# Gate phase G0 of a hybrid decoder layer: head outputs in pairs, merges and low weight halves on VectorE, projection passes ordered by token half

## The reference, cut to what matters

```python
h = rmsnorm(x, norm1_g)
proj = h @ w_in
...
y_a = silu(layernorm(ca, conf_ln_g, conf_ln_b)) @ conf_w_out
...
# ssd(), 16 heads, chunks of 128 tokens
decay = exp(where(causal, a_t[..., :, None] - a_t[..., None, :], -inf))
mix = cb[:, :, :, None] * decay
y_diag = einsum('bcgrij,bcjgrp->bcigrp', mix, xdt)
y_off = einsum('bclgn,bcgrpn,bclgr->bclgrp', cr, h_in, exp(a_cs))
...
gates = sigmoid(h @ w_gate + b_gate).reshape(n, t, 3, D_MODEL)
mixed = gates[:, :, 0] * y_a + gates[:, :, 1] * y_b + gates[:, :, 2] * y_c
x = x + mixed @ w_o
```

## Time and profile before

| | |
|---|---|
| median of 3 runs | 1107.23 us (1105.44 to 1108.96) |
| profiled execution | 1112.5 us, span 1110.6 us, mean clock of TensorE 0.961 |
| chain that ended last | TensorE 84% of the span, VectorE 12% |
| idle time of TensorE in stage G0, 314.2 to 435.46 us | 1.5 us |

### The profile page before, as it was taken

How to read it: one execution, slowest core, us unless ns; L and a number is a source line. 1 busy time by engine, 2 the same in 40 slices (tenths; PEclk the granted TensorE clock), 3 DMA queues, 4 the chain that set the end, 5 groups by cost and what they waited for, 6 DMA issues and landing times.

```text
span 1110.6 us, 19697 instructions
## 1 busy us (share of the span) xinstructions
PE 1060.9 (96%) x8110; PEld 1036.2 (93%) x8110; DVE 598.6 (54%) x834; ACT 374.0 (34%) x585; POOL 378.8 (34%) x255
## 2 busy tenths in 40 slices
PE   5999999899999999998999898999999999999996
PEld 5999989799998989988899898999999999999996
DVE  4799879966545676766301456543442003444454
ACT  4322256443524554311423212433332123333210
POOL 3200000000135444343466643544442445444340
PEclk9999899899999999886999999999999999999997
DMA  7322216212212314233224332133222233222122
GB/s 241 115 92 81 76 58 69 60 58 76 76 56 81 119 49 132 77 126 125 72 76 156 96 95 76 39 96 94 76 71 71 86 114 104 85 76 69 62 67 81
DMA packets 42461, 97.95 MB, mean 88 GB/s; under 512 B 14496, under 2 KB 15392, under 8 KB 42400
## 3 DMA queue, kind: packets, MB, share of 16 engines
q1 hardware_dynamic: 42400, 97.08, 28.9%
HBM read 89.13 MB, written 7.93 MB: 87 GB/s over the span
## 4 chain that ended last, share of the span: by engine, by line
PE 84%; DVE 12%; ACT 1%; POOL 1%; issue 1%; DMA 0%; SPq 0%; DVEq 0%; POOLq 0%
PE accs L379 75%; DVE ca L1324 2%; DVE temps L1387 2%; PE misc L1055 1%; DVE w_split L318 1%; PE misc L899 1%; PE misc L1058 1%; PE misc L893 1%; DVE temps L1696 1%; DVE branch L1801 1%; PE misc L906 1%; PE misc L1022 1%; PE misc L1068 1%; POOL w_split L318 0%; PE misc L1041 0%
## 5 line engine op out<-in xcount | busy, mean ns | idle before, releaser
L379 PE MATMUL accs<-h_split,w_split 128*128 128x272 f32 x4992 | 652.4, 293 | 7.1 <-POOL h_split L568 4.3
L379 PEld LDWEIGHTS accs<-h_split,w_split 128*128 128x128 f32 x4992 | 644.4, 192 | 12.5 <-POOL h_split L568 5.4
L318 POOL TENSOR_TENSOR w_split<-w_raw,w_split 128x1024 fp32r<-128x1024 f32 (+3 forms) x128 | 290.5, 2280 | 422.8 <-ACT w_split L313 422.8
L379 PE MATMUL accs<-branch,w_split 128*128 128x272 f32 x2208 | 290.4, 292 | 5.7 <-DVE branch L1801 3.6
L379 PEld LDWEIGHTS accs<-branch,w_split 128*128 128x128 f32 x2208 | 284.5, 191 | 9.7 <-DVE branch L1801 4.6
L313 ACT ACTIVATE w_split<-w_raw 128x1024 fp32r<-128x1024 f32 (+3 forms) x168 | 160.3, 963 | 201.2 <-PE accs L379 201.2
L1324 DVE SCALAR_TENSOR_TENSOR ca<-part,params,ca 128x512 f32<-128x512 f32 x120 | 83.5, 746 | 0.4
L1854 DVE TENSOR_TENSOR xbc<-accs,xbc 128x544 f32<-128x544 f32 x16 | 11.6, 725 | 94.7 <-PE accs L379 94.7
L1801 DVE TENSOR_TENSOR branch<-mixed,branch 128x544 fp32r<-128x544 f32 x8 | 16.3, 2100 | 80.9 <-ACT branch L834 80.9
L318 DVE TENSOR_TENSOR w_split<-w_raw,w_split 128x1024 fp32r<-128x1024 f32 (+1 forms) x40 | 44.9, 1126 | 27.2 <-ACT w_split L313 27.1
L682 ACT ACTIVATE temps<-accs 128x272 f32<-128x272 f32 (+2 forms) x102 | 25.5, 325 | 95.2 <-PE accs L379 95.2
(11 more groups left out here) (225 smaller groups left out, 777.0 us busy)
## 6 DMA issues: line engine op xcount, KB each, us to landing
w_raw<-in_ffn_w_up SPq DMA_DIRECT2D x44, 512.0 KB, 3.6
w_raw<-in_w_in_main SPq DMA_DIRECT2D x28, 512.0 KB, 3.5
w_raw<-in_w_gate SPq DMA_DIRECT2D x24, 512.0 KB, 3.6
w_raw<-in_ffn_w_down SPq DMA_DIRECT2D x16, 384.0 KB, 3.0
w_raw<-in_ffn_w_down SPq DMA_DIRECT2D x16, 320.0 KB, 2.9
xbc<-in_x SPq DMA_DIRECT2D x16, 272.0 KB, 5.3
w_raw<-in_w_in_z SPq DMA_DIRECT2D x8, 512.0 KB, 3.6
w_raw<-in_ssm_w_out SPq DMA_DIRECT2D x8, 512.0 KB, 3.7
```

Of the source, the lines that this page charges most:

```text
L318: e.tensor_tensor(w_split[:, s, 1, 0:n], w_raw[:, s, 0:n], w_split[:, s, 0, 0:n].bitcast(F32), ALU.subtract).then_inc(w_lo[s], 1)
L379: mm = pe.matmul(accs[:, a, half, 0:HALF], w_split[:, s, wp, k * P:(k + 1) * P], rhs(s, k, xp, half), start=(first and k == 0 and n == 0), ...
```

## The change

- `pe_quad` issues the three products of an input block for the first token half, then for the second.
- `y_pair` takes the place of `y_head`: per chunk the matmuls of the even and the odd head alternate. The table has heads in twos only, and the output comes two slots after the spread. Decays and decayed C have four buffers (`head_decay`, `c_dec`); the two new ones of `c_dec` lie in `u_sb`, where the second sample state goes, so its load moves behind the last head.
- VectorE reads G0's second accumulator itself and adds the product to `mixed` (`merge_second`), and makes the low weights of G0's quads 1 to 3 and of Z's quad 0 (`g0_slot`). GpSimd's merge of G0 and ScalarE's copy go.
- ScalarE takes the exponentials of the spreads of a slot first, then those of the differences.

```diff
-HEADS_AFTER = (0, 0, 0, 0, 0, 1, 1, 2, 1, 2, 1, 2, 2, 1, 2, 1)
+HEADS_AFTER = (0, 0, 0, 0, 0, 2, 2, 0, 2, 2, 2, 0, 2, 2, 2, 0, 0)
...
-        (c_dec,) = carve(ca_flat, (P, 2, SEQ))
+        c_dec = [half[:, r] for half in (carve(ca_flat, (P, 2, SEQ))[0], carve(u_flat[:, D:2 * D], (P, 2, SEQ))[0])
+                 for r in range(2)]
...
+        def head_decay(h):
+            return T(2 + h % 4, SEQ)
...
-                    for n, (wp, xp) in enumerate(((0, 0), (0, 1), (1, 0))):
-                        for half in range(2):
+                    for half in range(2):
+                        for n, (wp, xp) in enumerate(((0, 0), (0, 1), (1, 0))):
...
             load_h0(0)
-            load_h0(1)
             load_phase(sp, "Z")
             sp.wait_ge(sem("y_head"), HEADS)
+            load_h0(1)
...
             for s in range(SLOTS):
                 split_lo(pool, ph["G0"], 0, s)
-            merge("G0", 0)
...
-                    elif g != 2:
+                    elif g == 1:
                         wait(act, sem("merged"), j + n0)
...
                 for h in groups[4 * i + s]:
                     act.wait_ge(sem("diff"), h + 1)
-                    act.activation(T(4 + h % 2, SEQ), T(4 + h % 2, SEQ), ACT.Exp).then_inc(sem("pair_decay"), 1)
-                    if h >= 2:
-                        act.wait_ge(sem("y_head"), h - 1)
-                    act.activation(c_dec[:, h % 2], misc[:, h % 2], ACT.Exp).then_inc(sem("a_exp"), 1)
+                    if h >= 4:
+                        act.wait_ge(sem("y_head"), h - 3)
+                    act.activation(c_dec[h % 4], misc[:, h % 2], ACT.Exp).then_inc(sem("a_exp"), 1)
+                for h in groups[4 * i + s]:
+                    act.activation(head_decay(h), head_decay(h), ACT.Exp).then_inc(sem("pair_decay"), 1)
...
+            def y_pair(h0):
+
+                b0, pair = 2 + (h0 // 2) % 2, (h0, h0 + 1)
+                if h0 == 0:
                     pe.wait_ge(sem("chunk_state"), 2 * NCH)
+                if h0 >= 4:
+                    pe.wait_ge(sem("y_sum"), h0 // 2 - 1)
+                pe.wait_ge(sem("mix_head"), h0 + 2)
+                pe.wait_ge(sem("c_decayed"), h0 + 2)
                 for c in range(NCH):
                     cols = slice(c * CH, (c + 1) * CH)
+                    for h in pair:
+                        rows = slice((h % 2) * HD, (h % 2 + 1) * HD)
+                        mm = pe.matmul(misc[rows, b0, cols], xdt[:, c, h * HD:(h + 1) * HD],
+                                       head_decay(h)[:, cols], start=True, stop=(c == 0))
                     if c:
+                        for h in pair:
+                            rows = slice((h % 2) * HD, (h % 2 + 1) * HD)
+                            mm = pe.matmul(misc[rows, b0, cols], h_chunk[:, c - 1, h * HD:(h + 1) * HD],
+                                           c_dec[h % 4][:, cols], start=False, stop=True)
...
-                    for h in heads[k - 1] if k else ():
-                        y_head(h)
+                    for h in heads[k - 2] if k >= 2 else ():
+                        if h % 2 == 0:
+                            y_pair(h)
...
+            def merge_second(j):
+
+                p = ph["G0"]
+                dve.wait_ge(acc_free[0], p.pair0 + j + 1)
+                dve.wait_ge(acc_full[1], p.pair0 + j + 1)
+                dve.tensor_tensor(halves(T(j % 2)), acc(1), halves(T(j % 2)), ALU.mult).then_inc(acc_free[1], 1)
+                dve.wait_ge(acc_free[1], p.pair0 + j + 1)
+                dve.tensor_tensor(mixed[:, j], mixed[:, j], T(j % 2), ALU.add).then_inc(sem("merged"), 1)
+
+            def g0_slot(k):
+
+                i, s = divmod(k, SLOTS)
+                if s % 2:
+                    merge_second(2 * i + s // 2)
+                lo(*(("G0", i + 1) if i + 1 < ph["G0"].quads else ("Z", 0)), s)
+
             for c in range(NCH):
                 chunk_state(c)
                 if c < 2:
                     x_to_end(c + 2)
+                g0_slot(c)
...
+            for k in range(4, 4 * SLOTS):
+                for h in head_groups()[k]:
+                    diffs(h)
+                g0_slot(k)
+                for h in head_groups()[k]:
+                    mix_head(h)
+                y_sums(k)
+            y_sums(4 * SLOTS)
```

More of the change, by code:

```diff
@@ L609, in _ @@
             lo_odd("ssm", parts_of(ssm_at))
-            merge("G1", 8)
+            merge("G1")
             pool_phase("WO", nothing)
@@ L1196, in between @@
                     if (i, s) == (0, 0):
-                        for h in heads[-1]:
-                            y_head(h)
+                        for h in heads[14]:
+                            if h % 2 == 0:
+                                y_pair(h)
                     if (i, s) == (0, 1):
@@ L1665, in diffs, with mix_head @@
                 ins_.then_inc(sem("diff"), 1)
+            def mix_head(h):
+                dve.wait_ge(sem("pair_decay"), h + 1)
+                dve.tensor_tensor(head_decay(h), head_decay(h), cbm[:, h // 8], ALU.mult).then_inc(sem("mix_head"), 1)
+                dve.wait_ge(sem("a_exp"), h + 1)
+                dve.tensor_tensor(c_dec[h % 4], c_dec[h % 4], xbc[:, 10 + h // 8, 0:SEQ], ALU.mult)\
+                    .then_inc(sem("c_decayed"), 1)
             def y_sum(j):
@@ L1672, in y_sum, with y_sums @@
                     .then_inc(sem("y_sum"), 1)
-            before = ()
-            for group in [g for g in head_groups() if len(g)] + [()]:
-                for h in before:
+            def y_sums(k):
+                for h in head_groups()[k - 2]:
                     if h % 2:
                         y_sum(h // 2)
-                for h in group:
+            for k in range(4, 4 * SLOTS):
+                for h in head_groups()[k]:
                     diffs(h)
-                for h in group:
-                    dve.wait_ge(sem("pair_decay"), h + 1)
-                    dve.tensor_tensor(T(4 + h % 2, SEQ), T(4 + h % 2, SEQ), cbm[:, h // 8], ALU.mult)\
-                        .then_inc(sem("mix_head"), 1)
-                    dve.wait_ge(sem("a_exp"), h + 1)
-                    dve.tensor_tensor(c_dec[:, h % 2], c_dec[:, h % 2], xbc[:, 10 + h // 8, 0:SEQ], ALU.mult)\
-                        .then_inc(sem("c_decayed"), 1)
-                before = group
+                g0_slot(k)
[3 more added lines that the diff above has]
+            y_sums(4 * SLOTS)
             def y_times_z(b):
```

24 lines of the change are left out of this document (7 added, 17 removed).

## The result

| | before | after |
|---|---|---|
| median of 4 runs | 1106.37 us (1105.44 to 1108.96) | 1091.92 us (1087.12 to 1093.18) |
| profiled execution | 1112.5 us, span 1110.6 us, mean clock 0.961 | 1092.1 us, span 1090.3 us, mean clock 0.967 |

The ratio is 0.9854 with a 95% interval of 0.9826 to 0.9881: faster by 14.5 us at the medians. The forecast was 12 us and 1095, the range 1089 to 1108. The two profiled spans differ by 20.3 us, since the traced execution of before stood 6.1 us above the median of its runs in this table, and that of after 0.2.

A forecast was written before the change was run, and what follows sets the result against it. TensorE, busy 1060.9 of 1110.6 us, was taken as the bound. Gains of 10.8 + 0.6 + 1.2 = 12.6 us, less half a microsecond, gave 12 off the 1107.2 median: 1095 us, range 1089 to 1108.

The forecast's parts named there:

- Outputs in pairs: G0 stage, TensorE: alternating two heads' 28 records makes a pair take 1.64 us; 23.9 to 13.1 us, gain 10.8.
- its rival: Head outputs in G0: alternating column halves brings no overlap, a pair takes 3.2 us, kernel 1107 us; chance 0.07.
- Spreads: G0 stage, TensorE: eight double spreads replace six lone and five double ones, 5.8 to 5.2 us, gain 0.6.
- The wait ahead of line 1055: G0 stage: TensorE's waits before head outputs, 1.5 us in all, 1.2 of it for VectorE's line 1685.
- Two slots of lag: G0 stage: output two slots after its spread gives VectorE some 10 us; gain 1.2 us, bounds 0 and 1.5.
- table of slots 8 to 11: Tightest place in G0: VectorE has 25.2 us of work against TensorE's 26.1; the two slots of lag cover it.
- Merges and low halves on VectorE: G0 stage: 27.8 us added, 15.5 back, VectorE 89 us, hidden beside TensorE; booked 0, 3 us at the bad end.
- The rival with VectorE as the bound: G0 stage: VectorE's operations stay long, stage 126 us against 121.3, kernel 1112; deciding multiplication average about 1.02 us; chance 0.07.
- Passes ordered by token half: All 7200 projection matmuls: three passes in a row into one PSUM bank, each matmul still 0.125 us; taken as 0.
- the bounds were 58 us either way: Bank-order rival, projections: 12 ns on 4800 matmuls, kernel 1037 or 1153 us; chances 0.05 faster, 0.05 slower.
- The half microsecond taken off for late slots: G0 stage: half a microsecond subtracted from the 12.6 us sum for late slots, leaving 12.
- Z keeps its waits: Phase Z, behind the stage: VectorE and TensorE keep their offsets from the last pair, and TensorE's small waits stay.

The follow-up runs named there:

- e5_pair_in_turn: The changed kernel with the two heads of a pair issued one after the other again: 1098.84 us, ratio 0.9922 to the kernel before.
- e8_z_low_on_dve: The changed kernel with the low weight halves made during Z moved from GpSimd to VectorE too: 1084.73 us, ratio 0.9801 to the kernel before.
- e7_lag_one: The changed kernel with a pair's output one slot after its spread instead of two: 1116.28 us, ratio 1.0079 to the kernel before.

## Why the prediction was right, and where not

**Outputs in pairs** (10.8 us, the whole sum nearly): right in mechanism and size. A pair takes 1.68 us for the 1.64 assumed, so the term is 23.9 less 13.4, 10.5. The alternation alone is worth 6.9 us at the medians and 9.1 by the rows; the other 1.4 come from the new table, in which no head stands alone (eight twos in turn would take 22.6). The Trainium skill (TensorEngine Tiling (Array Packing), Theoretical Speedup) gives up to twice the rate where a dimension is 64 or less; 2.82 over 1.68 is 1.68 times, and a record every 54 ns for one every 110 is 2.0 times. The Trainium skill (TensorE: Matmul & The Clock Gate, Part 3) ties the overlap of weight loads to different row groups; by that rule alone, from which the prediction made its rival, e5_pair_in_turn would have been level with after. The same section also lists three matmuls in different column tiles at 2.38 times the speed, which the rival left out and which agrees in kind with these rows: here the streams differ in their columns only.

**Spreads** (0.6): as forecast, 0.65 us for two. **The wait ahead of line 1055** (1.5 in all, 1.2 booked): gone.

**Two slots of lag**: mis-sized. I priced it at the 1.2 us of waits that the kernel before had, but the lag is what makes pairs pay: with one slot the new kernel takes 24.4 us more than with two, 15.8 of them waits and some 8 the lower clock behind these. The step that failed is that a wait of the old design was taken as the price of the lag in the new one. The prediction's own table of slots 8 to 11 held the better answer: a pair's 6.2 us of VectorE work, with a merge and a low half, doesn't fit between a spread and an output one slot later, which is 3.3 us when that slot is a conf slot.

**Merges and low halves on VectorE** (0, with 3 us at the bad end): right, and with more room than I gave it. VectorE was busy for 81.5 us, not 89. Before's 76.7 plus the 27.8 added less 15.5 given back by the multiplications makes 89.0; another 7.5 us came back. Of these, 4.8 are two more groups that GpSimd had stretched and that I had left at their long times, here in before and then in after:

```profile
L1634 DVE TENSOR_TENSOR temps<-part,small 128x512 f32<-128x512 f32 x6 | 7.4, 1238 | 4.7 <-PE misc L1022 4.7
...
L1619 DVE TENSOR_TENSOR u_sb<-part,small 128x1024 f32<-128x1024 f32 x2 | 3.9, 1961 | 0.0
```

```profile
L1645 DVE TENSOR_TENSOR temps<-part,small 128x512 f32<-128x512 f32 x6 | 4.1, 689 | 3.6 <-PE misc L1026 3.6
...
L1630 DVE TENSOR_TENSOR u_sb<-part,small 128x1024 f32<-128x1024 f32 x2 | 2.4, 1216 | 0.0
```

The other 2.7 are a matter of counting: records of VectorE overlap a little, and a window counts the overlap once. Added up by line they are 79.5 us before and 87.0 after, where the windows have 76.7 and 81.5.

The rival with VectorE as the bound needed multiplications above 1.02 us; they took 0.69. Even 94.6 us of work were carried without a wait of more than 0.2 us.

**Passes ordered by token half** (0): the step that failed. The prediction named its own test, 798 matmuls in 100 us of projections; after has 802. It is small for one matmul, 0.9 ns, and 6.3 us for 7200 in the traces. I had looked for a price of the order of the 12 ns above 113, found none in two rows with another number format, and wrote 0; the bounds were 58 us either way, and nothing lay between. A price a tenth of that could not be seen in rows given to 10 ns, and the term should have carried a few us in both directions. The prediction had also said that any other number would break the forecast. That it held is luck in part: the number moved the good way, and this gain reaches the medians with only 1 to 3 of its 6 us.

**The sum** for the stage was 12.6 us. The rows give 10.5 + 0.6 + 1.5 = 12.6, plus 0.6 for the step of the stage's 624 projection matmuls: 13.2 of the 13.7 seen. The half microsecond taken off for late slots did not come due. The medians moved by 14.5 us, and 1091.9 lies 3.1 below the forecast of 1095. ScalarE's new order, the copies that it lost and the later load of the second state have no run of their own; the stage leaves half a microsecond for them. **Z keeps its waits**, as forecast, and e8_z_low_on_dve shows that they were the next thing to go after.

## What to carry to other kernels

Where two matmul streams write different column halves, alternate them, and give the engine that feeds both a lag long enough for the doubled bunch of work: without it the pairing costs more than it brings. The share of VectorE's time that GpSimd stretches is found by comparing one operation's length beside a GpSimd operation and without one; moving GpSimd's work to VectorE can then lower VectorE's busy time, but it pays only where TensorE waits for VectorE (Z: 4.7 us in the trace, 7.2 at the medians; G0 with its lag: nothing). A wait of TensorE can cost more than its length, by the clock behind it: 15.8 us of waits came with 8.2 us of slower work. And an edit of the innermost loop is multiplied by its count: 0.9 ns over 7200 matmuls is 6.3 us, half of the main term, though the medians showed no more than 3 of them.

## What the runs showed of the hardware

- Two float32 streams of 64 columns each, in different column halves, overlap throughout when they alternate: a record every 54 ns instead of every 110, and 1.68 us for a pair instead of 2.82 with the two streams in turn.
- The order of the six matmuls of an input block changes a matmul of 272 columns in fp32r by up to 1.1 ns (1989 to 2007 records in 250 us), which neither the banks nor the number of weight changes explains alone.
- In e7_lag_one four of the five waits of TensorE of 2.6 to 3.4 us were followed by a lower granted clock (0.71, 0.63, 0.72 and 0.82 over the next 6 to 9 us); the fifth, of 2.6 us, and two of 0.3 and 0.9 us were not (1.00). Behind one of 3.4 us a slot of 48 matmuls took 8.15 us at 0.73 instead of 6.18 at 1.00.
- A VectorE copy of 32 elements takes 0.18 us alone and 2.39 beside a low half on GpSimd, and it ends when that ends. The Trainium skill (SBUF — State Buffer, SBUF: two separate sides) says that the two engines share a pair of ports as an exclusive lock, held for a whole instruction; these rows agree.
